# Two sets of matmul operands begin 8 to 40 bytes further on in SBUF

## What is computed

```
p = rms_norm(x, g) @ w_in                      # 1024 x 5064: q, k, v, indexer, gates
o_a = sliding-window attention; o_b = attention over the top 256 keys of an indexer
x = x + rms_norm((sig(g_A)*o_a + sig(g_B)*o_b) @ w_o)
hid = square(relu(rms_norm(x) @ w_up))         # 1024 x 4096
y = x + rms_norm(hid @ w_down)                 # 4096 x 1024
```

## Time and profile before

| | |
|---|---|
| runs (3): lowest, median, highest | 1920.37, 1920.7, 1921.36 us |
| profiled execution: its time, its span | 1922.2 us, 1920.4 us |
| TensorE (PE) busy | 1872.4 us, 97% of the span, 11780 matmuls |
| DVE, ACT, POOL busy | 60%, 37%, 32% |
| mean granted TensorE clock | 0.993 of 2.4 GHz |

### The profile page before, as it was taken

How to read it: one execution, slowest core, us unless ns; L and a number is a source line. 1 busy time by engine, 2 the same in 40 slices (tenths; PEclk the granted TensorE clock), 3 DMA queues, 4 the chain that set the end, 5 groups by cost and what they waited for, 6 DMA issues and landing times.

```text
span 1920.4 us, 32592 instructions
## 1 busy us (share of the span) xinstructions
PE 1872.4 (97%) x11780; PEld 1772.4 (92%) x11780; DVE 1146.2 (60%) x2729; ACT 712.7 (37%) x1424; POOL 607.9 (32%) x460
## 2 busy tenths in 40 slices
PE   7999999999989999999999999999999999999995
PEld 6899999877778999999998889999999999999995
DVE  5259999999764666676664653333344443333336
ACT  5345554223344555555673342222222222222212
POOL 4225554134333344444351022222222222222214
PEclk9999999999999999999999999999999999999998
DMA  6433333333446444444323331111111111111104
GB/s 202 116 84 86 95 98 90 93 102 90 118 121 151 101 101 101 101 101 90 68 75 118 126 110 45 44 44 44 44 44 44 44 44 44 46 47 47 57 1 164
DMA packets 180396, 160.23 MB, mean 83 GB/s; under 512 B 101472, under 2 KB 148432, under 8 KB 180288
## 3 DMA queue, kind: packets, MB, share of 16 engines
q1 hardware_dynamic: 164816, 139.72, 25.7%
q10 hardware_dynamic: 15472, 19.09, 4.4%
HBM read 120.63 MB, written 39.27 MB: 83 GB/s over the span
## 4 chain that ended last, share of the span: by engine, by line
PE 92%; DVE 1%; DMA 1%; POOL 1%; SPq 1%; issue 0%; ACT 0%; DVEq 0%; POOLq 0%
PE ps L1076 22%; PE ps L2414 20%; PE ps L1886 20%; PE ps L1786 11%; PE ps L1762 6%; PE ps L1744 5%; PE ps L2133 5%; PE ps L1048 2%; DVE p_rstd L84 0%; DVE y L2363 0%; PE ps L2114 0%; PE ps L1980 0%; DMA dist_scr<-score 0%; PE ps L1103 0%; DMA q_raw<-q_scr 0%; DMA m_in<-merged_scr 0%
## 5 line engine op out<-in xcount | busy, mean ns | idle before, releaser
L2414 PE MATMUL ps<-hid_hi,weights 128*128 128x362 f32 (+1 forms) x1536 | 379.8, 327 | 0.0
L1886 PE MATMUL ps<-x2T_hi,weights 128*128 128x362 f32 (+1 forms) x1536 | 378.0, 326 | 0.0
L2351 DVE TENSOR_TENSOR total<-total,ps 128x364 f32<-128x364 f32 (+1 forms) x360 | 189.2, 532 | 139.8 <-PE ps L2414 139.8
L1886 PEld LDWEIGHTS ps<-x2T_hi,weights 128*128 128x128 f32 x1536 | 272.1, 188 | 0.1
L2414 PEld LDWEIGHTS ps<-hid_hi,weights 128*128 128x128 f32 x1536 | 270.4, 188 | 0.0
L1886 PE MATMUL ps<-x2T_lo,weights 128*128 128x362 f32 (+1 forms) x768 | 251.4, 327 | 0.0
L2414 PE MATMUL ps<-hid_lo,weights 128*128 128x362 f32 (+1 forms) x768 | 250.2, 326 | 0.0
L1076 PE MATMUL ps<-xT_hi,w 128*128 128x362 f32 (+1 forms) x960 | 246.0, 330 | 1.6 <-PEq L182 1.6
L2336 DVE TENSOR_TENSOR hidden<-hidden 128x362 f32<-128x362 f32 (+1 forms) x96 | 51.5, 537 | 293.5 <-ACT hidden L2311 293.5
L1873 POOL TENSOR_TENSOR weights<-down_raw,weights 128x512 fp32r<-128x512 f32 x64 | 83.8, 1312 | 380.8 <-ACT weights L1867 380.8
L1027 DVE MATCH_REPLACE8 score<-top,score 128x1024 f32<-128x1024 f32 (+5 forms) x208 | 199.3, 966 | 0.0
(11 more groups left out here) (197 smaller groups left out, 3325.6 us busy)
## 6 DMA issues: line engine op xcount, KB each, us to landing
q_raw<-q_scr SPq DMA_DIRECT2D x80, 256.0 KB, 5.2
w_raw<-in_w_in ACTq DMA_DIRECT2D x64, 256.0 KB, 3.0
up_raw<-in_w_up SPq DMA_DIRECT2D x64, 256.0 KB, 2.8
down_raw<-in_w_down SPq DMA_DIRECT2D x64, 256.0 KB, 2.6
gates<-gate_scr SPq DMA_DIRECT2D x34, 256.0 KB, 4.6
x_in<-in_x_prompt SPq DMA_DIRECT2D x16, 512.0 KB, 4.9
gate_scr<-stage SPq DMA_DIRECT2D x32, 256.0 KB, 3.1
q_scr<-stage SPq DMA_DIRECT2D x40, 181.0 KB, 3.1
```

Source lines behind the costliest of these rows:

```text
L1886: last = pe.matmul(ps[:, bank, 0:n], a[:, k, fs], b, start=(k == 0 and i == 0), stop=(k == KT - 1 and i == 2))
L2351: dve.tensor_tensor(out, out, more, ALU.add).then_inc(added, 1)
L2414: more = pe.matmul(ps[:, UP_BANKS + g % DOWN_BANKS, 0:n], a[:, f, cols], h, start=(f == 0 and i == 0), stop=(f == FT - 1 and i == 2))
```

## The change

Each of the six buffers `xT_hi`, `xT_lo`, `x2T_hi`, `x2T_lo`, `hid_hi`, `hid_lo` gets 16 fp32 (64 bytes) more room, and its data begins some elements after its first byte: 10 elements (40 bytes) for the x buffers, 2 elements (8 bytes) for the hid ones. No instruction is added or removed, no wait, no shape.

```diff
+def moved(tensor, first, rows, n):
+    return tensor[:, first:first + rows * n].rearrange("p (k n) -> p k n", n=n)
+
+LINE, X_FIRST, HIDDEN_FIRST = 16, 10, 2
-X_BYTES = 2 * 4 * KT * N_TOK
+X_BYTES = 2 * 4 * (KT * N_TOK + LINE)
...
-    out = place(nc, *first, FOOT, ("xT_hi", [P, KT, N_TOK], F32R), ("xT_lo", [P, KT, N_TOK], F32R), ("w", [P, 4, KT, 512], F32R),
+    out = place(nc, *first, FOOT, ("xT_hi", [P, KT * N_TOK + LINE], F32R), ("xT_lo", [P, KT * N_TOK + LINE], F32R), ("w", [P, 4, KT, 512], F32R),
...
-    return out | {"w_lo": out["w"][:, 0:4:2], "w_hi": out["w"][:, 1:4:2]}
+    return out | {"w_lo": out["w"][:, 0:4:2], "w_hi": out["w"][:, 1:4:2]} | \
+        {n: moved(out[n], X_FIRST, KT, N_TOK) for n in ("xT_hi", "xT_lo")}
...
-AFTER_TOTAL = UP_RAW_END + 4 * (2 * D + 2 * 364 + 2 * FT * N_QUERY + KT * N_QUERY)
+AFTER_TOTAL = UP_RAW_END + 4 * (2 * D + 2 * 364 + 2 * (FT * N_QUERY + LINE) + KT * N_QUERY)
...
-        hid_hi = sb("hid_hi", [P, FT, N_QUERY], F32R)
-        hid_lo = sb("hid_lo", [P, FT, N_QUERY], F32R)
+        hid_hi = moved(sb("hid_hi", [P, FT * N_QUERY + LINE], F32R), HIDDEN_FIRST, FT, N_QUERY)
+        hid_lo = moved(sb("hid_lo", [P, FT * N_QUERY + LINE], F32R), HIDDEN_FIRST, FT, N_QUERY)
...
-            x2T = [ctx.enter_context(nc.sbuf_tensor(n, [P, KT, N_QUERY], F32R)) for n in ("x2T_hi", "x2T_lo")]
+            x2T = [moved(ctx.enter_context(nc.sbuf_tensor(n, [P, KT * N_QUERY + LINE], F32R)), X_FIRST, KT, N_QUERY)
+                   for n in ("x2T_hi", "x2T_lo")]
```

## The result

The changed kernel takes 1940.03 us (median of 5 runs, 1939.6 to 1941.02), the kernel before 1921.2 us (5 runs, 1920.37 to 1922.41). The ratio is 1.0097, with a 95% interval of 1.0086 to 1.0109. Slower was right; the forecast was +7.6 us and it is +18.8 us, beyond the upper end of the range, 1931.5 us.

The account below looks back on a forecast made before the run. The prediction took the tensor engine's matmul stream as the bound; its terms -0.1 + 3.3 + 3.0 + 0.1 + 0.3 + 1.0 = +7.6 us gave 1920.7 + 7.6 = 1928.3 us, range 1913.8 to 1931.5 us.

Parts of the forecast that it names:

- The bound: Whole kernel: tensor engine busy 97% of the span, so changes in matmul distance enter the time one to one.
- The mechanism: Matmul streams: fast needs few 64-byte pieces and a steady place against the stationary operand; the change gives first, takes second.
- the test blocks: MLP up block 2 and down block 1: forecast slower, by +3.3 and +3.0 us, from 160.2 and 160.6 ns.
- The value of a block with 362 columns, 164.5 ns: MLP up and down blocks 1 and 2: all go to 164.5 ns, bounds 160.2 and 166.2; -0.1, +3.3, +3.0, +0.1 us.
- Blocks of 364 columns don't change: MLP block 0, up and down: stays at 166.7 and 166.9 ns, 0 us; bounds -5.0 us each and +0.3.
- Output mix: Output mix: one of three terms changes its place against the stationary operand; +1.0 us, half of a possible +2.1.
- Projection and xT stationary: Feature-major projection stays out of step, 0 us; matmuls with xT stationary, slices touching nine pieces for eight, +0.3 us.
- Rival (c): Matmuls with xT stationary: a nine-piece slice costs one step in each of 1080, +7.2 us, 1928 us; chance 0.07.
- Rival (a): MLP: piece count alone decides, so 362-column blocks run at 160.2 to 160.6 ns; -6.3 us, 1914.4 us; chance 0.32.
- Rival (b): MLP blocks: gains and losses cancel or the moving address matters less; within 3.8 us of 1920.7; chance 0.20.

Follow-up runs that it names:

- the map: Behind the kernel before, added streams of 24 matmuls sweep the starts of moving, lo and stationary operands; one run each: 2458.44, 2457.19 and 2455.78 us.
- Start places alone: Changed kernel with 256 bytes of room per buffer instead of 64, same moved starts, hi and lo in step modulo 256 bytes; 1929.17 us, ratio 1.0043.
- the kernels of the first table: Four follow-up kernels varying start places, hi-lo distance or place of buffers, against the kernel before at 1921.45 us: 1929.17, 1930.21, 1921.25 and 1933.52 us.
- in step, other places: Changed kernel with 256 bytes of room per buffer and data starting at 42 (x) and 18 (hid) columns, hi and lo in step; 1921.25 us, ratio 1.0001.
- the streams in threes: Behind the kernel before, one stream at each start 0 to 62, then two at 22 or 4; second took mostly 163.3, sometimes 166.7 ns at 22, 160.0 at 4.
- place against `weights`: Kernel before with 64 bytes put behind `weights`, so all buffers behind it move by one piece, hi and lo in step; 1933.52 us, ratio 1.0067.

## Why the prediction was right in direction and too small

- **The bound.** Confirmed. PE's distances go one to one into the time, no other engine counts: +17.5 us of PE busy, +17.4 us of time.
- **The mechanism (a fast stream needs few pieces, and a place against the stationary operand that stays the same from matmul to matmul; the change takes the second).** Half right. That a step between hi and lo costs is shown: up block 2 goes from 160.5 to 165.5 ns when x2T_lo alone moves, and the map has 166.1 against 164.9 ns and no start at 160. But the two conditions aren't enough, and the test blocks lost their 160 ns by something else. "Start places alone" keeps hi and lo in step and has up block 2 and down block 1 on 23 pieces, and they take 166.6 and 169.6 ns. The new starts are enough to slow them; the step adds nothing to them at these starts (166.7 and 167.0 in the changed kernel). The forecast's direction is right, its reason for these two blocks is not the one at work, and that part is luck.
- **The value of a block with 362 columns, 164.5 ns: the step that failed.** Terms forecast -0.1, +3.3, +3.0, +0.1 = +6.3 us; measured +1.4, +4.5, +4.7, +1.0 = +11.6 us. The four ran at 166.3, 166.7, 167.0 and 166.3 ns, at or just above what was given as the upper bound (166.2). I had called 164.5 the state "in which most streams are", from two blocks of the MLP that were in step, and there is no one such state: over 32 starts the map has values from 160.0 to 168.9 ns, with 166.7 the commonest. The argument had named the projection, 166.2 ns, as its example of a place that walks; taking that row gives (1.6 + 6.0 + 5.6 + 1.8) x 0.768 = +11.5 us for the four, within 0.1 us of the measured sum. That this row fits so well is partly luck: in the projection hi and lo are in step (xT_lo lies 138 x 256 bytes behind xT_hi) and the place walks from row to row only, and three of the four blocks get to 166.6 ns or more with hi and lo in step and nothing walking.
- **Blocks of 364 columns don't change: wrong.** Forecast 0 with +0.3 as upper bound; measured +1.8 and +1.2 us (169.1 and 168.8 ns). Three places at 167 were read as a wall. The map has 163.3, 165.0, 166.7, 168.3 and 173.3 ns at 364 columns, so it was a common value with others on both sides. Start places alone even gained 2.3 us in up block 0.
- **Output mix:** forecast +1.0, bound +2.1, measured +1.6 us, two rows at 231.3 ns for 227.0. In the kernels of the first table it moves only in those that shift it modulo 256 bytes. That the place counts is right; that only the term with `weights` would pay is not, as the distances behind all three kinds of matmul went from 227 or 228 to 232 ns.
- **Projection and xT stationary:** forecast 0 and +0.3, measured +0.7 and +0.7. Rival (c), 6.67 ns for a slice over nine pieces, is excluded: 232.9 ns, not 238.
- **Rival (a), the number of pieces:** fallen. All four 362-column blocks have 23 pieces after the change and none is at 160; 64 bytes behind `weights` leaves the pieces alone and costs 12 us.
- **Rival (b), gains and losses cancel:** not in this change; it happened in another kernel, "in step, other places" (1.0001).

Together: forecast 6.3 + 0 + 1.0 + 0.3 = 7.6; measured 11.6 + 3.0 + 1.6 + 1.4 = 17.6 us. Of the 10 us between them 5.3 are the value, 3.0 the blocks of 364 columns, 0.6 the output mix and 1.1 the projection with the gate chunks. The last 1.2 us up to 18.8 lie between this sum and the medians. The stated range ended at 1931.5 us, 2.0 us under the 1933.5 that its own working gives, without a reason; the measured time lies above both.

Open: no rule is known that gives the rate of a place from the addresses; the map is measured and not explained. Why down block 1 of "start places alone" is at 169.6 ns where the map has 161.7 was not tried; that the past of a stream can do such a thing is shown, by the streams in threes and by down block 0, but not that it did so there. And "place against `weights`" costs 12.1 us by the medians and 10.1 us between the profiled executions: the MLP's two lines are 8.6 us of these, the output mix 1.3, and all others together 0.2. The 2.0 us between the two figures were not followed.

## What to carry to other kernels

In this kernel's full streams, with a weight load for each matmul, the distance hangs on where both operands begin modulo 256 bytes. Keep the copies that alternate in a stream (hi and lo here) in step modulo 256 bytes, and let padding be a multiple of 256 bytes when nothing but the padding is meant. Then sweep the start, since the good places were found by a map and not by a rule: 5 of 1921 us came from it. Being in step is no guarantee: the new starts alone, in step, cost 7.7 us. And when the rows show two values for one instruction and no rule that separates them, the commoner value is no forecast: the bounds are the answer until a sweep over the one variable has been run.

## What the hardware showed that I had not expected

- The distance of identical matmuls at 362 columns ranges from 160.0 to 168.9 ns with the moving start alone, at 364 from 163.3 to 173.3, with a period of 256 bytes (64 columns). Starts on a multiple of 16 bytes are not better than others: their mean is 164.7 ns, that of all starts 164.9. The Trainium skill, "SBUF — State Buffer", section on the port swizzle, says that each crossing to a new 16-byte line costs something; the prediction's inference from it, that such a start should be the good one, is not borne out by the map.
- Several steady rates for one place: at 22 the same stream runs at 160.2 (in the kernel before), 163.3 or 166.7 ns, by what ran ahead of it; at 4 it ran at 160.0 behind all 32 starts.
- 364 columns can be as fast as 163.3 ns, and 340 columns take 153.3 ns at start 4. The Trainium skill, "TensorE: Matmul & The Clock Gate", section on the back-to-back issue gap, gives N/2.4 + 2.5 ns for an isolated matmul, by estimate 144.2 ns for 340 columns and 153.3 for 362, and says that a stream with weight loads is quicker than that at 512 columns. The best streams here take 153.3 ns at 340 and 160.0 at 362 columns, and at 512 columns 227.0 to 232.9 ns, where the formula gives 215.8 by estimate: they are slower than the formula, not quicker.
